# Fewer places for the small products of a gated linear recurrence, and a delta rule whose steps stand one unit later

## The reference

```python
# first layer: gated delta rule, 8 heads of 128, chunks (the kernel takes chunks of 128 in two of 64)
low = jnp.where(strict, einsum(kb, k) * decay, 0.0)
sol = triangular_solve(low + I, [v * beta, kb * exp(gc)])       # (I + low)^-1
v_new = u_i - w_i @ state;  o_i = q_i @ state + a_i @ v_new     # over chunks
# second layer: HGRN2, 16 heads of 128
f = lower_bound + (1 - lower_bound) * sigmoid(f_raw);  k = 1 - f
attn[t, s] = sum_d q[t, d] * k[s, d] * prod(f[s+1..t, d])       # s <= t
o = attn @ v;  y = rms_norm(o) * silu(z)
```

## Time and profile before

| | |
|---|---|
| median of 3 runs | 951.3 us (950.97 to 952.26) |
| profiled execution: its time, its span | 952.88 us, 951.1 us |
| TensorE busy | 919.6 us, 97% |
| GpSimd, ScalarE, VectorE busy | 71%, 52%, 49% |
| first layer's recurrence | about 75 to 310 us |
| second layer's recurrence | about 386 to 630 us |

### The profile page before, as it was taken

How to read it: one execution, slowest core, us unless ns; L and a number is a source line. 1 busy time by engine, 2 the same in 40 slices (tenths; PEclk the granted TensorE clock), 3 DMA queues, 4 the chain that set the end, 5 groups by cost and what they waited for, 6 DMA issues and landing times.

```text
span 951.1 us, 19421 instructions
## 1 busy us (share of the span) xinstructions
PE 919.6 (97%) x7694; PEld 845.9 (89%) x7694; DVE 468.2 (49%) x967; ACT 498.5 (52%) x702; POOL 673.7 (71%) x486
## 2 busy tenths in 40 slices
PE   5899899999999999999999999999999999999997
PEld 5899899998998889999999999888897889998886
DVE  3448855368453253666676666616646352221004
ACT  3575432574335465655765656555567356554441
POOL 3787656556565697967766776668798559889983
PEclk9999999999999999999999999999999999999999
DMA  5759356556544555745444554455663337666641
GB/s 176 216 198 172 100 142 107 133 135 110 128 128 118 204 176 157 211 148 152 136 131 143 151 153 133 138 192 164 182 207 111 99 105 220 195 188 202 205 133 45
DMA packets 133299, 146.12 MB, mean 154 GB/s; under 512 B 11022, under 2 KB 100056, under 8 KB 133208
## 3 DMA queue, kind: packets, MB, share of 16 engines
q1 hardware_dynamic: 131224, 140.64, 51.8%
q10 hardware_dynamic: 1984, 4.24, 1.3%
HBM read 143.81 MB, written 1.05 MB: 152 GB/s over the span
## 4 chain that ended last, share of the span: by engine, by line
PE 83%; DVE 7%; POOL 3%; issue 3%; ACT 2%; DMA 1%; SPq 1%; DVEq 0%; ACTq 0%; POOLq 0%
PE dense L560 23%; PE dense L562 22%; PE dense L561 22%; PE bank L935 2%; POOL wlo L535 2%; DMA raw<-in_w_in_even_dram 1%; POOL wlo L534 1%; PE bank L830 1%; PE bank L826 1%; PE bank L845 1%; PE dense L629 1%; PE bank L992 1%; ACT whi L1190 1%; DVE cv L1776 1%; PE bank L943 1%
## 5 line engine op out<-in xcount | busy, mean ns | idle before, releaser
L535 POOL TENSOR_TENSOR wlo<-raw,whi 128x512 fp32r<-128x512 f32 (+1 forms) x263 | 410.9, 1570 | 28.0 <-ACT whi L1190 28.0
L534 POOL TENSOR_TENSOR wlo<-raw,whi 128x512 fp32r<-128x512 f32 x199 | 258.1, 1297 | 218.8 <-ACT whi L1190 218.5
L1190 ACT ACTIVATE whi<-raw 128x1024 fp32r<-128x1024 f32 x264 | 275.4, 1058 | 251.9 <-PE dense L562 199.5
L560 PE MATMUL dense<-x_hi,whi 128*128 128x256 f32 x1232 | 358.6, 291 | 10.3 <-POOL wlo L529 5.4
L561 PE MATMUL dense<-x_lo,whi 128*128 128x256 f32 x1232 | 346.1, 281 | 0.0
L562 PE MATMUL dense<-x_hi,wlo 128*128 128x256 f32 x1232 | 345.9, 281 | 0.0
L560 PEld LDWEIGHTS dense<-x_hi,whi 128*128 128x128 f32 x1232 | 234.1, 190 | 18.4 <-issue 8.9
L561 PEld LDWEIGHTS dense<-x_lo,whi 128*128 128x128 f32 x1232 | 235.2, 191 | 1.8 <-issue 1.7
L562 PEld LDWEIGHTS dense<-x_hi,wlo 128*128 128x128 f32 x1232 | 234.0, 190 | 0.0
L560 PE MATMUL dense<-whi,ya_hi 128*128 128x512 f32 x192 | 78.0, 406 | 1.0 <-issue 0.8
L562 PE MATMUL dense<-whi,ya_lo 128*128 128x512 f32 x192 | 75.0, 391 | 0.0
(11 more groups left out here) (331 smaller groups left out, 1403.0 us busy)
## 6 DMA issues: line engine op xcount, KB each, us to landing
raw<-in_w_in_odd_dram SPq DMA_DIRECT2D x64, 512.0 KB, 3.8
raw<-in_w_in_even_dram SPq DMA_DIRECT2D x32, 512.0 KB, 6.6
raw<-in_w_in_even_dram SPq DMA_DIRECT2D x64, 256.0 KB, 4.5
raw<-in_mlp_w_up_dram SPq DMA_DIRECT2D x32, 512.0 KB, 4.0
raw<-in_mlp_w_down_dram SPq DMA_DIRECT2D x32, 512.0 KB, 4.6
raw<-in_w_out_even_dram SPq DMA_DIRECT2D x16, 512.0 KB, 3.8
raw<-in_w_pl_gate_dram SPq DMA_DIRECT2D x16, 512.0 KB, 4.4
raw<-in_w_out_odd_dram SPq DMA_DIRECT2D x16, 512.0 KB, 4.2
```

The costliest lines, as they stand in the source:

```text
L534: pool.tensor_tensor(wlo[:, slot, 0:half], unit_slot(u)[:, 0:half], whi[:, slot, 0:half].bitcast(F32), ALU.subtract)
L535: pool.tensor_tensor(wlo[:, slot, first:2 * half], unit_slot(u)[:, first:2 * half], whi[:, slot, first:2 * half].bitcast(F32), ALU.subtrac ...
L560: pe.matmul(out_, lh, rh, start=start, stop=False, skip_group_check=True)
L1190: act.activation(whi[:, u % NSPL, :], unit_slot(u), ACT.Copy).then_inc(hi_done, 1)
```

## The change

In the delta rule, step 4 and all after it stand one unit later (`GDN_BEHIND`). In HGRN2 the small work of a pair moves from r = 5, 6, 8, 10, 11, 12, 13, 15 to r = 6, 8, 10, 11, 14, 16 (the last pair: 12 and 14 for the last two). As 14 and 16 of a pair are 6 and 8 of the next, four places are left in eight units, from seven. The diagonal, the halves and the chunk product write `SB[1]` in place of `SB[0]`; the scaled operands of the chunk product go to two new tiles, `kx` and `qx`, made already at r = 10 ahead of the picks (`hg_reach`), and the chunk product is cut into eight matmuls of 64 output rows and 64 columns in place of two of 128 by 128. The diagonal's picks follow the key scaling of the first level.

```diff
+HG_LAST = 11
+HG_OUT = [14] * (HH // 2 - 1) + [12]
...
-GDN_BEHIND = [0, 1, 2, 4, 6] + list(range(7, 19)) + [19, 20, 22, 24]
+GDN_BEHIND = [0, 1, 2, 4] + list(range(7, 20)) + [20, 21, 23, 25]
...
@@ TensorE: hg_diagonal
                 if p > 0:
+                    pe.wait_ge(hg_picked, 5 * p)
                     pe.wait_ge(hg_cross, p)
@@ hg_blocks
-                pe.wait_ge(hg_picked, 5 * p + n + 1)
+                if n > 0:
+                    pe.wait_ge(hg_picked, 5 * p + n + 1)
@@ hg_halves
-                pe.wait_ge(hg_picked, 5 * p + 4)
+                pe.wait_ge(hg_picked, 5 * p + 1)
@@ hg_across
                 pe.wait_ge(hg_ranked, 5 * p + 5)
-                pe.wait_ge(hg_picked, 5 * p + 5)
                 for i in range(2):
-                    last = pe.matmul(SB[0][:, i * P:(i + 1) * P], tokens_of(hk, p % 2, i, 0), tokens_of(q0, p % 2, i, 1), start=True, stop=True)
+                    first = 2 * P + i * P
+                    for half, queries in enumerate((tokens_of(q0, p % 2, i, 1)[:, 0:64], qx[:, i, :])):
+                        cols = slice(first + 64 * half, first + 64 * half + 64)
+                        pe.matmul(SB[1][0:64, cols], kx[:, i, :], queries, start=True, stop=True)
+                        last = pe.matmul(SB[1][64:P, cols], tokens_of(hk, p % 2, i, 0)[:, 64:P], queries, start=True, stop=True)
@@ VectorE: hg_blocks, after the keys are scaled
                 if n == 0:
                     free("qf", p)
+                    hg_diagonal(p)
+                if n == 2:
+                    hg_reach(p)
@@ VectorE: new, and what is left of hg_halves
+            def hg_reach(p):
...
+                link(vec.tensor_tensor(kx[:, :, :], k, spread(f[:, :, 0, 1], 64), ALU.mult))
+                link(vec.tensor_tensor(qx[:, :, :], q, spread(f[:, :, 1, 0], 64), ALU.mult), hg_ranked)
...
+                vec.wait_ge(hg_cross_mm, p + 1)
+                o = four(AA[0:64, p % 2, :])[:, :, 64:P]
+                link(vec.tensor_copy(o, SB[1][0:64, 0:256].rearrange("p (u c) -> p u c", u=4)), hg_picked)
+                vec.tensor_copy(CR[:, p % 2, :], SB[1][:, 2 * P:4 * P]).then_inc(hg_cross, 1)
@@ ScalarE: squares; VectorE: gain; and so on for the root (HG_OUT + 3) and the split (HG_OUT + 4)
-                    if r == 14:
+                    if r == HG_OUT[p] + 1:
                         hg_squares(p)
...
-                    if g - 8 * p == 14:
+                    if g - 8 * p == HG_OUT[p] + 1:
```

More of the change, by code:

```diff
@@ L234, in build @@
             sqo = sb("sqo", [P, 2 * T], stack=ph)
+            kx = sb("kx", [P, 2, 64], stack=ph)
+            qx = sb("qx", [P, 2, 64], stack=ph)
             yg = sb("yg", [P, 2 * T], stack=ph)
@@ L921, in hg_diagonal @@
                         rows = slice(64 * b, 64 * b + 64)
-                        last = pe.matmul(SB[0][rows, u * 64:(u + 1) * 64], tokens_of(hk, p % 2, u // 2, u % 2)[:, rows],
+                        last = pe.matmul(SB[1][rows, u * 64:(u + 1) * 64], tokens_of(hk, p % 2, u // 2, u % 2)[:, rows],
                                          tokens_of(q0, p % 2, u // 2, u % 2)[:, rows], start=True, stop=True)
@@ L940, in hg_halves @@
                 pe.wait_ge(hg_ranked, 5 * p + 4)
-                pe.wait_ge(hg_picked, 5 * p + 4)
+                pe.wait_ge(hg_picked, 5 * p + 1)
                 for u in range(4):
-                    last = pe.matmul(SB[0][0:64, u * 64:(u + 1) * 64], tokens_of(hk, p % 2, u // 2, u % 2)[:, 0:64],
+                    last = pe.matmul(SB[1][0:64, u * 64:(u + 1) * 64], tokens_of(hk, p % 2, u // 2, u % 2)[:, 0:64],
                                      tokens_of(q0, p % 2, u // 2, u % 2)[:, 64:P], start=True, stop=True)
@@ L977, in _ @@
                     r = g - 8 * p
-                    if r == 5:
+                    if r == HG_BLOCKS[0]:
                         hg_diagonal(p)
@@ L981, in _ @@
                         hg_blocks(p, HG_BLOCKS.index(r))
-                    if r == 11:
+                    if r == HG_LAST:
                         hg_halves(p)
+                        hg_across(p)
                 for p in range(HH // 2):
                     r = g - 8 * p
-                    if r == 12:
-                        hg_across(p)
-                    if r == 13:
+                    if r == HG_OUT[p]:
                         hg_out(p)
-                    if r == 15:
+                    if r == HG_OUT[p] + 2:
                         pe.wait_ge(hg_yg, p + 1)
@@ L1565, in _ @@
                     r = g - 8 * p
-                    if r == 14:
+                    if r == HG_OUT[p] + 1:
                         hg_squares(p)
-                    if r == 16:
+                    if r == HG_OUT[p] + 3:
                         hg_root(p)
-                    if r == 17:
+                    if r == HG_OUT[p] + 4:
                         hg_high(p)
@@ L2118, in hg_diagonal @@
                     mask = ident[rows, rows].unsqueeze(1).broadcast_to([64, 4, 64]).bitcast(I32)
-                    link(vec.copy_predicated(four(AA[rows, p % 2, :])[:, :, rows], mask, SB[0][rows, 0:256].rearrange("p (u c) -> p u c", u=4)),
+                    link(vec.copy_predicated(four(AA[rows, p % 2, :])[:, :, rows], mask, SB[1][rows, 0:256].rearrange("p (u c) -> p u c", u=4)),
                          hg_picked if b else vec_chain)
@@ L2156, in hg_blocks @@
                         pairs(p, 32)
+            def hg_reach(p):
+                if p > 0:
+                    vec.wait_ge(hg_cross_mm, p)
+                f = decays(p, 64).rearrange("p (i t h) -> p i t h", i=2, t=2)
+                k = hk[:, p % 2, :].rearrange("p (i c) -> p i c", i=2)[:, :, 0:64]
+                q = q0[:, p % 2, :].rearrange("p (i c) -> p i c", i=2)[:, :, P + 64:T]
+                link(vec.tensor_tensor(kx[:, :, :], k, spread(f[:, :, 0, 1], 64), ALU.mult))
+                link(vec.tensor_tensor(qx[:, :, :], q, spread(f[:, :, 1, 0], 64), ALU.mult), hg_ranked)
             def hg_halves(p):
-                par = p % 2
                 vec.wait_ge(hg_level_mm, 5 * p + 5)
[L2162 to L2168, removed]
+                vec.wait_ge(hg_cross_mm, p + 1)
+                o = four(AA[0:64, p % 2, :])[:, :, 64:P]
+                link(vec.tensor_copy(o, SB[1][0:64, 0:256].rearrange("p (u c) -> p u c", u=4)), hg_picked)
+                vec.tensor_copy(CR[:, p % 2, :], SB[1][:, 2 * P:4 * P]).then_inc(hg_cross, 1)
+                settle(hg_cross)
             vec.wait_ge(consts_loaded, 48)
@@ L2181, in _ @@
                         hg_gate(p)
-                    if r == 5:
-                        hg_diagonal(p)
                     if r in HG_BLOCKS:
                         hg_blocks(p, HG_BLOCKS.index(r))
-                    if r == 11:
+                    if r == HG_LAST:
                         hg_halves(p)
```

## The result

The changed kernel takes **956.35 us** (median of 20 runs, 949.82 to 959.52), the kernel before in the same series 951.15 (20 runs, 948.45 to 955.73): 1.0045 times as long, 95% interval 1.003 to 1.0059. 944.9 was forecast, faster. The profiled execution took 957.34 us, 4.46 more than that of before. One profiled execution is not the median: the trace tells where time lies, the medians tell how much it is.

A forecast was written before the change was run, and what follows sets the result against it. TensorE, busy 97% of the span, was taken as the bound. Gains of 4.0 (delta rule, first half), 0.4 (second half) and 2.0 (HGRN2), together 6.4 us, off the median 951.3 gave 944.9 us; range 942.2 to 947.4.

The forecast's parts named there:

- Step 6 then starts at 111.9 + ...: Delta rule, first half: step 6 starts at 116.0, one unit more done than before at 117.26; gain 4.0 us.
- The 4.67 us that I took for lost: Delta rule, first half: time lost up to step 5's start at 113.17, waiting and half clock together.
- rival (B): Delta rule's waits return one place later, VectorE being full from step 2 to 6; half of 4.4 lost, 947.1, 10%.
- The price: Second half, step 1: 1.5 us later from ScalarE, 3.2 us standing still, then half clock costing 1.7 more.
- The gain: Second half, step 4: 3.73 us lost before, its wait gone with a unit ahead; net of slips 0.4 us.
- the price of 0.61 for sixteen records: HGRN2: cut chunk product as 16 records of the diagonal's form, 0.69 less a 0.08 tail.
- The cut product's price: HGRN2: 0.61 us for the cut chunk product, where the uncut one costs 0.45.
- (A): Second half: clock doesn't drop at step 1, or ScalarE is less late; 943.2 us, 25%.
- (C): HGRN2 gives nothing, as places at r = 8 or 11 wait for more VectorE instructions; 946.9 us, 5%.
- (D): HGRN2, r = 8: VectorE's line after the first blocks makes TensorE wait; 956.9 at 1.5 us a pair, 3%.
- (E): No change: second half loses about 2, HGRN2 0.5, added to rival (B); 951 us, 2%.
- The forecast for the slow side: Whole kernel: chance of 0.03 that the change measures slower.

The follow-up runs named there:

- the cut alone: Kernel before with only HGRN2's chunk product cut into eight matmuls of 64 output rows and 64 columns, old place and bank: 958.82 us, ratio 1.008.
- +192: Kernel before with 192 more instructions on TensorE's queue that only wait for what has already come: 956.37 us, ratio 1.0035.
- +480: Kernel before with 480 more instructions on TensorE's queue that only wait for what has already come: 961.41 us, ratio 1.0113.

## Why the prediction was wrong

**Delta rule, first half (-4.0 forecast, -1.4).** The step that failed is "Step 6 then starts at 111.9 + ...": it lets TensorE run on through the next unit as soon as step 4 no longer waits. Step 4's wait did go, and steps 5 and 6 came without one. But unit 24, now ahead of step 4, needs banks that VectorE frees behind the same step 3. The old wait for step 3's result had hidden this second one. The wait was moved by one place and lengthened from 2.1 and 0.9 to 3.8 in one piece, and the half clock came with it. That is shown: freeing the banks earlier takes 4.5 us off. The 4.67 us that I took for lost had a second flaw: about 1.7 of them were half clock, and that is not part of every execution. In three kernels with step 4 where it was (the cut alone, +192, +480) the same waits of 1.9 to 2.1 and 0.8 us were not followed by it, and blocks 20 to 27 took 32.04, 31.95 and 31.85 us, no more than the 31.93 after the change. So even the 1.4 is not shown to be a gain. It is rival (B) with a cause that I had not named; a line of three semaphores had to be followed for the dense unit as well as for the small work.

**Delta rule, second half (-0.4 forecast; +3.9 from block 27 to 74, of which 0.5 lies ahead of block 46).** The price was right: step 1 idles 3.17 us where 3.2 was forecast, 2.6 more than before, the clock drops, and block 46 costs 4.25 more, so the half clock took 1.6 where 1.7 was forecast; with step 20 back it is 7.18 again. A reading was off: the idle stretches at step 4 of this half are 1.18 and 0.77 us, not 1.3 and 0.9. The gain was the part that failed, for two reasons. Behind the moved step 4 unit 51 waits 1.81 us at line 1680, for `ya_low(3)`, the same mechanism as in the first half, and line 830 waits 0.7 us a little later. And the gain was capped by what was there: blocks 51 to 55 took 20.54 us before and 18.18 after, 2.4 less and not 3.7. Here too the half clock counts: where it didn't follow the old step 4, the same blocks took 18.94 to 19.31, and where it followed the wait at unit 51 in changed kernels, 19.01 to 19.13. A further 1.5 us are spread over blocks 55 to 74, in pieces of which I have settled none.

**HGRN2 (-2.0 forecast, -4.1).** The step that failed is the price of 0.61 for sixteen records whatever stands behind them: the mechanism was right, and two terms were mis-sized. Places of a pair cost 7.50 us before and 2.82 + 1.87 + 1.02 + 1.28 = 6.98 after. Joining the diagonal and the blocks saved 0.35, not 0.20: sixteen records of one 64-row form followed by others of that form take 0.51, and I had priced them with what they need ahead of a 128-wide one. Halves and chunk saved 0.17, not 0.05, probably for the same reason. The cut product's price held only where it stands alone: 0.61 and going in and out, 0.36 a pair, against 0.37 measured in the kernel that has the cut alone. Behind the halves, as in the change, it cost next to nothing: that place takes 1.27 us cut and 1.25 uncut. The Trainium skill (TensorEngine Tiling (Array Packing), Theoretical Speedup) gives up to 2 times for sizes of 64, by which the cut product would cost no more than the whole one. The trace agrees to 0.02 us where other products of 64 rows stand ahead, and doesn't for the place of its own (0.82 against 0.45).

**The first 90 us (0 forecast, +5.95 in the profile, about +5 in the medians).** I let the sum begin where the code differs: the step that failed is that the cut's price was looked for in HGRN2 alone, and the stretch ahead of block 20 had no term. The 48 matmuls that the cut adds cost 0.02 us a pair where they stand in the change, 0.3 us over all of HGRN2 (291.35 against 291.01), and some 4 to 5 us elsewhere, by the profiles at the other end of the program. In the profile of the change a part of the 5.95 is its two stretches of half clock, worth up to 1.6 each by the price above. That the length of TensorE's program brings this about is shown by waits that do no work, and by its absence when the cut is taken back (956.35 and 950.52, of which 0.3 are the uncut product's own). Why a longer program makes DMA slower from the first 10 us on is not shown by anything here. The Trainium skill (Runtime: NRT & Kernel Launch, Instruction fetch mechanics) says that each engine's code streams in blocks of 16 KiB and that crossing one is mostly hidden. The trace agrees on the block (1.00 MB in 61 packets). It also shows no more idle time of TensorE without a releaser after than before (0.8 us, once, in both), but a 62nd packet is not free in the total.

Of the rivals, (A) is refuted (the clock dropped), (C) too, and the one on the slower side, (D), named a place where nothing waits. (E) had a second half that turns into a loss, of 2 us where 3.9 came, beside a loss in HGRN2 that didn't come. The forecast for the slow side was 3%; what decided the early loss was in none of them.

**What beats both kernels** is the merged places with the uncut product, the sums of keys freed first and step 20 left where it was: 944.66 us.

## What to carry to other kernels

When small work is moved one unit later, ask of the dense unit that now stands ahead of it what it needs itself, banks above all, and whether VectorE frees them behind the very step that was waited for; an instruction of 0.17 us that frees a bank belongs ahead of 6 us of work that doesn't. Count the instructions that an edit adds to TensorE, and compare the number of instruction packets with that of the kernel before: where it grows and DMA sets the start, measure the edit again with the same number of instructions. When one profile stands for a kernel whose runs spread by 1%, check its early part against a second kernel that differs only late. Don't book a stretch of half clock as a gain before a second profile of the same code shows it again.

## What the runs showed of the hardware

- 192 instructions on TensorE's queue that do nothing, all from block 141 on (596 us), made a kernel of 952.6 us 3.7 us slower; 96 of them, or 222 on VectorE's queue, did not. All ten kernels with 62 or 63 instruction packets came to block 20 at 86.6 to 94.0 us in their profiles, all eight with 61 at 84.2 to 86.1. DMA moved 1.56 to 1.67 MB in the first 10 us with 62 or 63 instruction packets, 1.70 to 1.82 with 61.
- Standing still for 3.6 to 3.8 us at unit 24 and for 3.2 us at step 1 was followed by the 1.2 GHz level in four profiles of four each, for 3.4 us and once for 6.8. Standing still for 1.8 us at unit 51 was followed by it in three profiles and not in three others, and the waits of 1.9 to 2.1 and 0.8 us at the old step 4 were followed by it in some profiles and not in others.
- A chunk product of 128 x 128 for each of two heads, cut into eight of 64 x 64 outputs, took 0.82 us at a place of its own in place of 0.45. At the end of a place of other 64-row products the place took 1.27 us with it and 1.25 with the uncut one.
- Sixteen records of a 64-row product take 0.51 us ahead of another 64-row product and 0.61 ahead of a 128-wide one.
- The picks of line 2149 took 0.44 to 0.46 us at the first level of blocks and 0.22 to 0.24 at the other two, with GpSimd busy or idle.
